# w_ff_out loaded on ScalarE's queue, two tiles of w_ff_in loaded ahead, and evictions placed between two high/low parts, in a float32 decoder block

## The chip, the cores and the metric

One core of one Trainium2 chip. The metric is the device time of one execution of the whole kernel in microseconds, the median of the runs.

## The reference

One decoder block on 512 tokens of width 1024, in float32. The part that this change touches is the last, the feed-forward stage with 4096 hidden columns:

```python
hf = rms_norm(x, norm_ff_pre)
ff = jnp.square(jax.nn.relu(hf @ w_ff_in)) @ w_ff_out
return x + rms_norm(ff, norm_ff_post)
```

Ahead of it stand the input projection, a chunked spatial gating, a windowed attention, their gated merge, and the product with w_o, whose normed result is added to x (the "mixing stage" below).

## The kernel before

It is written for each engine by hand: one program per engine, with semaphores between them, so the order on an engine is the order of the code.

**Three products for one.** To keep float32 accuracy on TensorE, each operand is split into a high part (a rounding to `F32R`, made by ScalarE: `w_hi`, `actB_hi`, `op_hi`) and a low part (the rest, made by VectorE: `w_lo`, ...). The helper `product` issues three 128x512 matmuls: high by high, high by low, low by high (L1368 to L1370). Weights come as 512 KB tiles into four buffers `w_raw[0..3]`; their high and low parts live in rings of four, `w_hi` and `w_lo`. Each such pair is a unit; `hi_made` and `lo_made` count them. Unit r may only be made once TensorE is through with unit r - 4, so a high part is always made four units ahead: when TensorE has finished unit r, `hi_ahead(r)` and `lo_ahead(r)` make unit r + 4.

**The feed-forward stage** runs in four chunks of 1024 hidden columns. A chunk has 22 units:

- eight units of "up": `acc` bank = one tile of w_ff_in by the activations (24 matmuls). ScalarE evicts each with a relu (L874), VectorE squares it (L1240) and forms sums and differences of the four column pairs. In chunk 0 the up units use four banks, later two.
- fourteen units of "down", 12 matmuls each: seven products P1, P5, P6, P7, P4, P3, P2 (the order of `PRODUCTS`) with two halves h each. It is a 2x2 block scheme with seven products in the place of eight. Their right operands are pieces of w_ff_out in `down_raw`, or differences T1 to T4 of such pieces, formed by VectorE in `weight_sum` (L1218) and kept in `down_raw` or in `t_raw`, which is another name of `w_raw[2:4]`.

P5, P7 and P3 stay in banks of their own over all chunks. P1, P6, P4 and P2 (`ROTATING`) take turns in banks `acc[0:2]`: each must be evicted into `sum1`, `sum6`, `sum4` or `sum2` before the next of them starts, and P2's before the next chunk's first up unit. Between P1 and P6, P6 and P4, P4 and P2 stands one resident product of two units, between P2 and the next chunk nothing. In chunk 0 ScalarE evicts them (copies at L894), in chunks 1 and 2 VectorE adds them (L1305), in the last chunk VectorE merges them with the other products (`merge`, L1224, and L1332, L1353). TensorE waits for that in `bank_free` and ahead of the up units (`taken`, counted per bank).

**What follows what around the change.** At every product, ScalarE calls `hi_ahead` for both halves and then evicts; VectorE calls `lo_ahead` for both halves, with the sums T2b, T3b, T4a, T4b among them, and then evicts or merges. Behind P2 the units made are the up units 2 and 3 of the next chunk.

Since T1, T2 and T4 occupy `w_raw[2:4]` during a chunk, the tiles of w_ff_in of chunks 1 to 3 all use buffers 0 and 1, one after the other: tile m waits for the low part of tile m - 2 (`load_up`). The blocks of w_ff_out, two rows of tiles or 1 MB each, are issued by SP between them (`load_down`, L506): behind each of tiles 2 to 5 of a chunk one block. All loads of weights are on SP's queue; ScalarE's queue carries two small loads at the start of the kernel.

In the mixing stage ScalarE makes the squares of the first half (`mix_square`, L806), then works through `WO_ORDER["act"]`.

Of the kernel before, what the change touches and what calls it, by code (L numbers as in the profile page):

```python
# [41 lines left out]
P = 128  # L42
D = 1024
# [205 lines left out]
def hybrid_block(nc, x, positions, w_in, ln_v_gain, ln_v_bias, w_spatial, b_spatial, sinks, w_a, w_b,  # L249
# [11 lines left out]
    with ExitStack() as ctx:  # L261
# [163 lines left out]
        def _(sp):  # L425
# [82 lines left out]
            for m in range(SLOTS):  # L508
                load_up(m)
            load_up(4)  # L510
            load_up(5)
            sp.wait_ge(a_lo, GROUPS)
            load_down(0, 0)
            load_down(0, 1)
            load_up(6)
            load_down(0, 2)
            load_up(7)
            load_down(0, 3)
            sp.wait_ge(pe_done, UNIT_DONE[U_FF - 1])
            sp.dma_start(g_ff_post[:], norm_ff_post[0:1, :].to_broadcast([P, D])).then_inc(g_ff_in, 16)  # L520
            for c in range(1, CHUNKS):
# [108 lines left out]
        def _(act):  # L630
# [171 lines left out]

            def mix_square(part, t, src, signal):
# [63 lines left out]
            for c in range(CHUNKS):  # L867
# [816 lines left out]
```

## Time and profile before

| | us |
|---|---|
| median of 3 runs (lowest to highest) | 811.88 (810.15 to 816.54) |
| the profiled execution | 810.79 |
| its span, first to last instruction | 809.1 |
| TensorE busy in it | 772.7 |
| VectorE busy | 529.7 |
| ScalarE busy | 364.8 |

The profile is of one execution. "PE" is TensorE, "DVE" VectorE, "ACT" ScalarE, "SPq" and "ACTq" are DMA issues on the queues of SyncE and ScalarE. In a timeline, an x with a number joins instructions of one kind; the time in brackets is how long the engine was idle before, with what released it. The granted clock is a share of 2.4 GHz.

### The profile page before, as it was taken

How to read it: one execution, taken by the hardware profiler on the slowest of the kernel's cores; microseconds unless marked ns; L12 is line 12 of the kernel's file. 1: busy time of each engine (PE TensorE's matmuls, PEld its weight loads, DVE VectorE, ACT ScalarE, POOL GpSimd, SP SyncE). 2: the span in 40 equal slices, each digit the busy share in tenths (PEclk: the TensorE clock that was granted, in tenths of full speed). 3: DMA queues.
4: the chain of work that ended last, by engine and by line, in shares of the span. 5: the costliest groups of instructions: out<-in, count | busy, mean ns of one | idle time of the engine just before them, and what ended most of it. 6: DMA issues, size and time to landing. Idle time of an engine off the chain costs nothing.

```text
span 809.1 us, 9921 instructions
## 1 busy us (share of the span) xinstructions
PE 772.7 (96%) x3640; PEld 645.1 (80%) x3640; DVE 529.7 (65%) x883; ACT 364.8 (45%) x609; POOL 58.3 (7%) x110
## 2 busy tenths in 40 slices
PE   7999999999999999999999999989996999979994
PEld 6888888888887888888888988778784887768873
DVE  5624667777775329766547698437962588547897
ACT  4523656656566552322245455334531344324532
POOL 3000000123222003000002000000000000000002
PEclk9999999999999999999999999999997999999998
DMA  8333222222123522353332440272008200270002
GB/s 286 127 108 89 69 79 78 79 79 79 53 79 107 179 79 86 96 211 109 114 89 82 168 141 1 99 242 76 1 0 308 83 26 1 81 257 27 0 1 104
DMA packets 91580, 80.29 MB, mean 99 GB/s; under 512 B 2832, under 2 KB 77584, under 8 KB 91536
## 3 DMA queue, kind: packets, MB, share of 16 engines
q1 hardware_dynamic: 90864, 79.70, 30.6%
q8 instruction: 27, 0.44, 0.2%
q14 instruction: 17, 0.14, 0.1%
q10 hardware_dynamic: 672, 0.01, 0.0%
HBM read 77.60 MB, written 2.10 MB: 99 GB/s over the span
## 4 chain that ended last, share of the span: by engine, by line
PE 86%; DVE 7%; DMA 3%; ACT 2%; issue 1%; SPq 0%; POOL 0%; DVEq 0%; POOLq 0%; ACTq 0%
PE acc L1368 25%; PE acc L1370 25%; PE acc L1369 25%; DMA w_raw<-in_w_ff_in 2%; PE aux L1370 2%; PE aux L1369 2%; PE aux L1368 2%; DVE w_lo L1201 1%; DMA w_raw<-in_w_in 1%; PE aux L1555 1%; PE aux L1481 1%; PE aux L1480 1%; PE aux L1490 1%; DVE w_lo L1197 1%; DVE sum L1224 1%; PE acc L1509 1%
## 5 line engine op out<-in xcount | busy, mean ns | idle before, releaser
L1368 PE MATMUL acc<-actB_hi,w_hi 128*128 128x512 f32 (+1 forms) x544 | 210.0, 386 | 17.4 <-DVE sum L1305 13.2
L1370 PE MATMUL acc<-actB_hi,w_lo 128*128 128x512 f32 (+1 forms) x544 | 207.2, 381 | 0.0
L1369 PE MATMUL acc<-actB_lo,w_hi 128*128 128x512 f32 (+1 forms) x544 | 207.1, 381 | 0.0
L919 DVE TENSOR_TENSOR w_lo<-w_raw,w_hi 128x1024 fp32r<-128x1024 f32 x72 | 87.8, 1223 | 83.9 <-ACT w_hi L636 83.1
L1368 PEld LDWEIGHTS acc<-actB_hi,w_hi 128*128 128x128 f32 x544 | 103.9, 191 | 37.1 <-DVE w_lo L1197 14.1
L1370 PEld LDWEIGHTS acc<-actB_hi,w_lo 128*128 128x128 f32 x544 | 103.7, 191 | 19.6
L1369 PEld LDWEIGHTS acc<-actB_lo,w_hi 128*128 128x128 f32 x544 | 104.0, 191 | 18.5
L636 ACT ACTIVATE w_hi<-w_raw 128x1024 fp32r<-128x1024 f32 x72 | 75.5, 1052 | 71.2 <-PE acc L1370 68.8
L1368 PE MATMUL acc<-w_hi,op_hi 128*128 128x512 f32 x160 | 62.5, 390 | 2.5 <-DVE sum L1305 1.3
L1368 PE MATMUL acc<-w_hi,actB_hi 128*128 128x512 f32 x160 | 62.7, 392 | 1.4 <-DVE actB_lo L929 1.3
L1370 PE MATMUL acc<-w_hi,op_lo 128*128 128x512 f32 x160 | 63.5, 397 | 0.0
L1369 PE MATMUL acc<-w_lo,op_hi 128*128 128x512 f32 x160 | 63.3, 396 | 0.0
L1370 PE MATMUL acc<-w_hi,actB_lo 128*128 128x512 f32 x160 | 62.3, 389 | 0.0
L1369 PE MATMUL acc<-w_lo,actB_hi 128*128 128x512 f32 x160 | 62.3, 389 | 0.0
L874 ACT ACTIVATE ff_act<-acc 128x512 f32<-128x512 f32 x32 | 19.1, 596 | 79.1 <-PE acc L1370 79.1
L1197 DVE TENSOR_TENSOR w_lo<-w_raw,w_hi 128x1024 fp32r<-128x1024 f32 x28 | 34.3, 1225 | 28.5 <-ACT w_hi L834 28.4
L1201 DVE TENSOR_TENSOR w_lo<-down_raw,w_hi 128x1024 fp32r<-128x1024 f32 x32 | 39.0, 1222 | 17.5 <-ACT w_hi L846 17.4
L1240 DVE TENSOR_TENSOR ff_act<-ff_act 128x512 f32<-128x512 f32 x32 | 22.0, 689 | 42.6 <-ACT ff_act L874 42.6
L846 ACT ACTIVATE w_hi<-down_raw 128x1024 fp32r<-128x1024 f32 x32 | 33.8, 1058 | 31.2 <-PE acc L1370 18.7
L745 ACT ACTIVATE probs<-scores_sb,neg_m 128x256 f32<-128x256 f32 (+1 forms) x64 | 30.1, 472 | 30.8 <-DVE sink_m L1068 30.8
L834 ACT ACTIVATE w_hi<-w_raw 128x1024 fp32r<-128x1024 f32 x28 | 29.6, 1056 | 30.4 <-DMA w_raw<-in_w_ff_in 21.0
L1368 PEld LDWEIGHTS acc<-w_hi,op_hi 128*128 128x128 f32 x160 | 30.7, 192 | 10.6 <-DVE w_lo L1201 2.1
(192 smaller groups left out, 1292.7 us busy)
## 6 DMA issues: line engine op xcount, KB each, us to landing
w_raw<-in_w_in SPq DMA_DIRECT2D x44, 512.0 KB, 3.8
w_raw<-in_w_ff_in SPq DMA_DIRECT2D x32, 512.0 KB, 4.1
down_raw<-in_w_ff_out SPq DMA_DIRECT2D x16, 1024.0 KB, 8.2
w_raw<-in_w_b SPq DMA_DIRECT2D x8, 512.0 KB, 3.6
w_raw<-in_w_a SPq DMA_DIRECT2D x8, 512.0 KB, 3.7
w_raw<-in_w_o SPq DMA_DIRECT2D x8, 512.0 KB, 3.7
x<-in_x SPq DMA_DIRECT2D x4, 512.0 KB, 7.4
x<-in_x SPq DMA_DIRECT2D x1, 2048.0 KB, 8.4
```

The lines of the kernel that those rows point to most:

```text
L636: nc.scalar.activation(w_hi[:, j], w_raw[:, j], ACT.Copy).then_inc(hi_made, 1)
L745: nc.scalar.activation(probs[:, h, off:], scores_sb[:, h, off:], ACT.Exp, bias=neg_m[:, h:h + 1], accum_out=denom[:, h:h + 1])
L834: nc.scalar.activation(w_hi[:, r % SLOTS], w_raw[:, j], ACT.Copy).then_inc(hi_made, 1)
L846: nc.scalar.activation(moving(w_hi, r % SLOTS), right_raw(name, h), ACT.Copy).then_inc(hi_made, 1)
L874: nc.scalar.activation(ff_act[:, m % 4], acc[:, bank], ACT.Relu).then_inc(relu_made, 1)
L919: nc.vector.tensor_tensor(w_lo[:, j], w_raw[:, j], w_hi[:, j].bitcast(F32), ALU.subtract).then_inc(lo_made, 1)
L1197: nc.vector.tensor_tensor(w_lo[:, r % SLOTS], w_raw[:, m if m < SLOTS else m % 2], w_hi[:, r % SLOTS].bitcast(F32), ALU.subtract).then_inc ...
L1201: nc.vector.tensor_tensor(moving(w_lo, r % SLOTS), right_raw(PRODUCTS[k], h), moving(w_hi, r % SLOTS).bitcast(F32), ALU.subtract).then_inc ...
L1240: nc.vector.tensor_tensor(f, f, f, ALU.mult).then_inc(sq_made, 1)
L1368: nc.tensor.matmul(o, a_hi, b_hi, start=first, stop=False)
L1369: nc.tensor.matmul(o, a_hi, b_lo, start=False, stop=False)
L1370: return nc.tensor.matmul(o, a_lo, b_hi, start=False, stop=last)
```

## The change

1. w_ff_out is issued from ScalarE. In chunk 0 two blocks go out before the squares of the mixing stage and two behind the last transposed tile; in chunks 1 to 3 all four behind the high part of tile 3, in front of the first relu.
2. Tiles 2 and 3 of w_ff_in of chunks 1 to 3 get buffers 2 and 3 (`up_slot`), free when the low parts of P4's two units of the chunk before are made. Tiles 4 and 5 then wait for tiles 0 and 1, tiles 6 and 7 for 4 and 5.
3. At every product an eviction stands between the two high parts (ScalarE) or the two low parts (VectorE). T3b and T4b stand behind the first low part. In the last chunk the merges of P1, P6, P7, P4 and P3 also stand between the two low parts; the gains of P4 stay behind both.

```diff
+def up_slot(m):
+
+    n = m % FF_UNITS
+    return n if n < SLOTS else n % 2
...
             def load_up(m):
-                if m < SLOTS:
+
+                c, n = divmod(m, FF_UNITS)
+                if n >= SLOTS:
+                    sp.wait_ge(lo_made, U_FF + ff_unit(m - 4 if n < 6 else m - 2) + 1)
+                elif c == 0:
                     slot_free(U_FF + m)
+                elif n < 2:
+                    sp.wait_ge(lo_made, U_FF + ff_unit(c * FF_UNITS - 2 + n) + 1)
                 else:
-                    before = m - 4 if m < 6 else m - 2
-                    sp.wait_ge(lo_made, U_FF + ff_unit(before) + 1)
-                load_columns(m if m < SLOTS else m % 2, w_ff_in_v, slice(m * P, (m + 1) * P))
-
-            def load_down(c, j):
-
-                if c:
-                    sp.wait_ge(lo_made, U_FF + item(c, 0))
-                elif j >= 2:
-                    sp.wait_ge(turned, T_FF + TT)
-                k = c * FF_UNITS + 2 * j
-                sp.dma_start(down_raw[:, j], w_ff_out_v[:, k:k + 2, :]).then_inc(down_loaded[j], 16)
...
+                    sp.wait_ge(lo_made, U_FF + product_item(c - 1, "P4", n - 2) + 1)
+                load_columns(up_slot(m), w_ff_in_v, slice(m * P, (m + 1) * P))
+
+            for c in range(CHUNKS):
                 for n in range(FF_UNITS):
                     load_up(c * FF_UNITS + n)
-                    if 2 <= n < 2 + PAIRS:
-                        load_down(c, n - 2)
...
+            def load_down(c, j):
+
+                k = c * FF_UNITS + 2 * j
+                act.dma_start(down_raw[:, j], w_ff_out_v[:, k:k + 2, :]).then_inc(down_loaded[j], 16)
+
+            act.wait_ge(a_lo, GROUPS)
+            load_down(0, 0)
+            load_down(0, 1)
+
...
+            act.wait_ge(turned, T_FF + TT)
+            load_down(0, 2)
+            load_down(0, 3)
+
...
                 for name in PRODUCTS:
-                    for h in range(2):
-                        hi_ahead(product_item(c, name, h))
+                    hi_ahead(product_item(c, name, 0))
                     if c == 0 and name in ROTATING:
                         dst = {"P1": sum1, "P6": sum6, "P4": sum4, "P2": sum2}[name]
                         for p in range(2):
                             act.wait_ge(pe_done, BANK_DONE[U_FF + product_item(c, name, 1), p])
                             nc.scalar.activation(dst[:, p], acc[:, p], ACT.Copy).then_inc(taken, 1)
+                    hi_ahead(product_item(c, name, 1))
+                    if name == "P2" and c < CHUNKS - 1:
+                        act.wait_ge(lo_made, U_FF + item(c + 1, 0))
+                        for j in range(PAIRS):
+                            load_down(c + 1, j)
...
-                    for h in range(2):
-                        at = FF_UNITS + 2 * PRODUCTS.index(name) + h
-                        for made in {8: ["T2b"], 9: ["T3b"], 10: ["T4a"], 11: ["T4b"]}.get(at, []):
-                            weight_sum(c, made)
-                        lo_ahead(item(c, at))
+                    at = FF_UNITS + 2 * PRODUCTS.index(name)
+                    for made in {8: ["T2b"], 10: ["T4a"]}.get(at, []):
+                        weight_sum(c, made)
+                    lo_ahead(item(c, at))
+                    for made in {8: ["T3b"], 10: ["T4b"]}.get(at, []):
+                        weight_sum(c, made)
...
+                    lo_ahead(item(c, at + 1))
+                    if last and name == "P4":
                         dve.wait_ge(ff_ready, 4)
```

On ScalarE, at the end of chunk 0 (P4, P3, P2) and the start of chunk 1, this stood there before; `w_hi<-w_raw` at L834 are the up tiles of chunk 1:

```order
L846 ACTIVATE w_hi<-down_raw 128x1024 x4
L894 ACTIVATE sum4<-acc 128x512 x2
L834 ACTIVATE w_hi<-w_raw 128x1024 x4
L894 ACTIVATE sum2<-acc 128x512 x2
L874 ACTIVATE ff_act<-acc 128x512
```

and this now (L854 and L842 are the old L846 and L834, L901 the old L894, L882 the old L874):

```order
L854 ACTIVATE w_hi<-down_raw 128x1024 x3
L901 ACTIVATE sum4<-acc 128x512 x2
L854 ACTIVATE w_hi<-down_raw 128x1024
L842 ACTIVATE w_hi<-w_raw 128x1024 x3
L901 ACTIVATE sum2<-acc 128x512 x2
L842 ACTIVATE w_hi<-w_raw 128x1024
L801 DMA down_raw<-in_w_ff_out 128x2x1024 x4
L882 ACTIVATE ff_act<-acc 128x512
```

One high part moved from in front of each pair of evictions to behind it, and four DMA issues came in before the first relu.

On VectorE, from P1 to the start of the next chunk, in chunk 1, this stood there before (L1218 are the sums T2b, T3b, T4a and T4b, L1201 and L1197 the low parts, L1305 the evictions):

```order
L1218 TENSOR_TENSOR w_raw<-down_raw,w_raw 128x1024
L1201 TENSOR_TENSOR w_lo<-w_raw,w_hi 128x1024
L1218 TENSOR_TENSOR down_raw<-down_raw 128x2x512
L1201 TENSOR_TENSOR w_lo<-w_raw,w_hi 128x1024
L1305 TENSOR_TENSOR sum1<-acc,sum1 128x512 x2
...
L1305 TENSOR_TENSOR sum4<-acc,sum4 128x512 x2
L1197 TENSOR_TENSOR w_lo<-w_raw,w_hi 128x1024 x4
L1305 TENSOR_TENSOR sum2<-acc,sum2 128x512 x2
L1240 TENSOR_TENSOR ff_act<-ff_act 128x512
```

and this now (L1230, L1213, L1209, L1318 and L1252 are the old L1218, L1201, L1197, L1305 and L1240):

```order
L1230 TENSOR_TENSOR w_raw<-down_raw,w_raw 128x1024
L1213 TENSOR_TENSOR w_lo<-w_raw,w_hi 128x1024
L1230 TENSOR_TENSOR down_raw<-down_raw 128x2x512
L1318 TENSOR_TENSOR sum1<-acc,sum1 128x512 x2
L1213 TENSOR_TENSOR w_lo<-w_raw,w_hi 128x1024
...
L1209 TENSOR_TENSOR w_lo<-w_raw,w_hi 128x1024 x3
L1318 TENSOR_TENSOR sum2<-acc,sum2 128x512 x2
L1209 TENSOR_TENSOR w_lo<-w_raw,w_hi 128x1024
L1252 TENSOR_TENSOR ff_act<-ff_act 128x512
```

The evictions of P1 stand one low part earlier, and so do those of P2.

## Rows read from the trace of the kernel before

**Rows 1.** The page: busy time of TensorE, its share of the span, instructions.
```profile
PE 772.7 (96%) x3640; PEld 645.1 (80%) x3640; DVE 529.7 (65%) x883; ACT 364.8 (45%) x609; POOL 58.3 (7%) x110
```

**Rows 2.** What TensorE waited for: us in total, times, longest us.
```profile
PE acc L1368 <- DVE sum L1305: 14.5, 4, 7.7
PE acc L1368 <- ACT sum L894: 4.2, 1, 4.2
...
PE acc L1368 <- DVE sum L1224: 1.2, 1, 1.2
```

**Rows 3.** Timeline of TensorE: start, duration, line, operation, [idle before, its releaser].
```profile
524.06 0.40 PE L1369 MATMUL acc<-w_lo,op_hi 128*128 128x512 f32 x1
524.29 0.40 PE L1370 MATMUL acc<-w_hi,op_lo 128*128 128x512 f32 x1
...
528.84 0.76 PE L1368 MATMUL acc<-actB_hi,w_hi 128*128 128x512 f32 x1 [4.15 <-ACT sum L894]
...
531.97 0.40 PE L1369 MATMUL acc<-actB_lo,w_hi 128*128 128x512 f32 x1
...
621.56 0.77 PE L1368 MATMUL acc<-actB_hi,w_hi 128*128 128x512 f32 x1 [7.74 <-DVE sum L1305]
...
627.62 0.39 PE L1370 MATMUL acc<-actB_hi,w_lo 128*128 128x512 f32 x1
...
713.35 0.77 PE L1368 MATMUL acc<-actB_hi,w_hi 128*128 128x512 f32 x1 [5.49 <-DVE sum L1305]
...
716.40 0.39 PE L1369 MATMUL acc<-actB_lo,w_hi 128*128 128x512 f32 x1
```

**Rows 4.** Stretches; behind busy times per engine: granted clock, DMA share, GB/s.
```profile
584.00:588.00 4.00, 3.36 (x15) 2.45 (x14) 4.00 (x5) 1.06 (x1) 0.00 (x0) 1.00 0.00 0
...
613.90:621.50 7.60, 0.00 (x0) 0.00 (x0) 2.35 (x4) 1.06 (x1) 0.00 (x0) 0.72 1.06 368
621.56:627.50 5.94, 5.94 (x14) 4.68 (x15) 0.45 (x1) 0.00 (x0) 0.00 (x0) 0.50 0.89 320
```

**Rows 5.** Timelines at the second boundary: ScalarE, then VectorE, then SP's queue.
```profile
608.37 1.06 ACT L834 ACTIVATE w_hi<-w_raw 128x1024 fp32r<-128x1024 f32 x1 [1.71 <-PE aux L1370]
...
618.50 1.06 ACT L834 ACTIVATE w_hi<-w_raw 128x1024 fp32r<-128x1024 f32 x1 [5.43 <-DMA w_raw<-in_w_ff_in]
...
620.73 1.28 DVE L1305 TENSOR_TENSOR sum<-acc,sum 128x512 f32<-128x512 f32 x2
...
611.13 0.58 SPq L506 DMA_DIRECT2D down_raw<-in_w_ff_out  x1
614.36 0.37 SPq L431 DMA_DIRECT2D w_raw<-in_w_ff_in  x1
```

**Rows 6.** Timelines at P6 of chunk 1: VectorE, then TensorE.
```profile
583.88 1.22 DVE L1201 TENSOR_TENSOR w_lo<-w_raw,w_hi 128x1024 fp32r<-128x1024 f32 x1
585.02 1.28 DVE L1305 TENSOR_TENSOR sum<-acc,sum 128x512 f32<-128x512 f32 x2
...
585.85 0.47 PE L1368 MATMUL acc<-w_hi,op_hi 128*128 128x512 f32 x1 [0.64 <-DVE sum L1305]
```

**Rows 7.** Timeline of VectorE in the last chunk.
```profile
777.84 1.23 DVE L1201 TENSOR_TENSOR w_lo<-w_raw,w_hi 128x1024 fp32r<-128x1024 f32 x1 [0.26 <-ACT w_hi L846]
...
783.32 1.23 DVE L1201 TENSOR_TENSOR w_lo<-down_raw,w_hi 128x1024 fp32r<-128x1024 f32 x1 [0.67 <-ACT w_hi L846]
...
798.97 0.68 DVE L1353 TENSOR_TENSOR sum<-acc,sum 128x512 f32<-128x512 f32 x1
```

**Rows 8.** The issues at L506 (min/median/max ns), their landing; timeline of ScalarE.
```profile
L506 SPq DMA_DIRECT2D down_raw<-in_w_ff_out x16: 469/582/2438, 440.6 to 713.0; - x16
...
DMA to landing us min/median/max: 6.1/8.2/10.3
...
421.18 0.60 ACT L806 ACTIVATE junk_wo<-acc 128x512 f32<-128x512 f32 x1 [0.84 <-PE acc L1370]
...
455.47 0.60 ACT L874 ACTIVATE ff_act<-acc 128x512 f32<-128x512 f32 x1 [4.72 <-PE acc L1370]
```

More of the change, by code:

```diff
@@ L99, in product_item, with up_loads @@
     return item(c, FF_UNITS + 2 * PRODUCTS.index(name) + h)
+def up_slot(m):
+    n = m % FF_UNITS
+    return n if n < SLOTS else n % 2
+def up_loads(m):
+    return U_FF // SLOTS + sum(up_slot(x) == up_slot(m) for x in range(m + 1))
 def ff_unit(m):
@@ L491, in load_up @@
             def load_up(m):
-                if m < SLOTS:
+                c, n = divmod(m, FF_UNITS)
+                if n >= SLOTS:
+                    sp.wait_ge(lo_made, U_FF + ff_unit(m - 4 if n < 6 else m - 2) + 1)
+                elif c == 0:
                     slot_free(U_FF + m)
-                else:
-                    before = m - 4 if m < 6 else m - 2
-                    sp.wait_ge(lo_made, U_FF + ff_unit(before) + 1)
-                load_columns(m if m < SLOTS else m % 2, w_ff_in_v, slice(m * P, (m + 1) * P))
-            def load_down(c, j):
-                if c:
-                    sp.wait_ge(lo_made, U_FF + item(c, 0))
-                elif j >= 2:
-                    sp.wait_ge(turned, T_FF + TT)
-                k = c * FF_UNITS + 2 * j
-                sp.dma_start(down_raw[:, j], w_ff_out_v[:, k:k + 2, :]).then_inc(down_loaded[j], 16)
[L508 to L521, printed above, removed]
+                elif n < 2:
+                    sp.wait_ge(lo_made, U_FF + ff_unit(c * FF_UNITS - 2 + n) + 1)
+                else:
+                    sp.wait_ge(lo_made, U_FF + product_item(c - 1, "P4", n - 2) + 1)
+                load_columns(up_slot(m), w_ff_in_v, slice(m * P, (m + 1) * P))
+            for c in range(CHUNKS):
                 for n in range(FF_UNITS):
                     load_up(c * FF_UNITS + n)
-                    if 2 <= n < 2 + PAIRS:
-                        load_down(c, n - 2)
+                if c == 0:
+                    sp.wait_ge(pe_done, UNIT_DONE[U_FF - 1])
+                    sp.dma_start(g_ff_post[:], norm_ff_post[0:1, :].to_broadcast([P, D])).then_inc(g_ff_in, 16)
             for n, t in enumerate((2, 3)):
@@ L826, in _ @@
                     hi_of(U_FF + t)
+            act.wait_ge(turned, T_FF + TT)
+            load_down(0, 2)
+            load_down(0, 3)
             def hi_up(m):
-                j = m if m < SLOTS else m % 2
-                act.wait_ge(w_loaded[j], 16 * (U_FF // SLOTS + 1 + (0 if m < SLOTS else (m - SLOTS) // 2 + 1)))
+                j = up_slot(m)
+                act.wait_ge(w_loaded[j], 16 * up_loads(m))
                 r = ff_unit(m)
@@ L1196, in lo_ahead @@
                     m = c * FF_UNITS + n
-                    nc.vector.tensor_tensor(w_lo[:, r % SLOTS], w_raw[:, m if m < SLOTS else m % 2],
+                    nc.vector.tensor_tensor(w_lo[:, r % SLOTS], w_raw[:, up_slot(m)],
                                             w_hi[:, r % SLOTS].bitcast(F32), ALU.subtract).then_inc(lo_made, 1)
@@ L1305, in _ @@
                             nc.vector.tensor_tensor(dst[:, p], acc[:, p], dst[:, p], ALU.add).then_inc(taken, 1)
-                    if not last:
-                        continue
-                    if name == "P1":
+                    if last and name == "P1":
                         merged_so_far()
@@ L1313, in _ @@
                             merge(sum6[:, p], acc[:, p], sum6[:, p], signal=taken)
-                    if name == "P6":
+                    if last and name == "P6":
                         for p in range(2):
@@ L1319, in _ @@
                         merge(sum1[:], acc[:, 2:4], sum6[:])
-                    if name == "P7":
+                    if last and name == "P7":
                         bank_done(name, 1)
@@ L1333, in _ @@
                             ins.then_inc(ff_ready, 1)
+                    if last and name == "P3":
+                        for p in range(2):
+                            bank_done(name, p)
+                            merge(sum1[:, p], aux[:, 2 + p], sum1[:, p], signal=ff_ready)
+                    lo_ahead(item(c, at + 1))
+                    if last and name == "P4":
                         dve.wait_ge(ff_ready, 4)
@@ L1339, in _ @@
                             gain(2 + p, sum4[:, p], 0, 2 + p)
-                    if name == "P3":
-                        for p in range(2):
-                            bank_done(name, p)
-                            merge(sum1[:, p], aux[:, 2 + p], sum1[:, p], signal=ff_ready)
+                    if last and name == "P3":
                         for p in range(2):
```

1 line of the change is left out of this document (removed).

## The prediction

> **What bounds the kernel now.** I read the page first, then what TensorE waits for, then the granted clock by stretches, then the timelines around the waits. TensorE is busy 96% of the span [rows 1]. What it waits for after the first 20 us is short [rows 2]: evictions of product banks into `sum` tiles, 14.5 us in 4 waits on VectorE (two at L1305 of about 0.64 us each, two large), 4.2 us in one wait on ScalarE (L894) and 1.2 us at L1224. The three large ones stand where a chunk of the feed-forward stage ends and the next begins: chunks 0 to 1, 1 to 2, 2 to 3. The timelines show 4.15, 7.74 and 5.49 us idle there, and behind each the matmuls start 0.43 us apart instead of 0.23 [rows 3].
>
> The clock explains the spacing: 0.50 granted (1.2 GHz) for the 5.94 us behind the second gap, against 1.00 (2.4 GHz) in a stretch with a 0.64 us gap [rows 4]. TensorE had been idle for 4 us and more before it fell, and stayed up through 0.64 us. The Trainium skill ("TensorE: Matmul & The Clock Gate", section "HAM oscillation — how this bites in real kernels") says that a TensorE left waiting for a DMA falls back to half clock and starts cold. By that rule, the trace agrees, at 0.50 behind all three large gaps. Were the small gaps left by this change to cost the clock too, by the price of the shortest stretch at half clock (1.5 us) twice, the sum below would be 3.0 us smaller.
>
> Why is the eviction late? Follow the second boundary [rows 5]. The chain reads backwards: TensorE starts at 621.56, 0.83 us behind the start of the P2 evictions (620.73); those stand on VectorE behind the low part of tile 3 of the next chunk, this behind its high part on ScalarE (618.50), this behind its DMA (idle 5.43 us, released by w_ff_in), and that DMA was only issued at 614.36, in a buffer that was free only then, behind 1 MB blocks of w_ff_out on the same queue (611.13). TensorE's own operands (tile 0) were ready long before. So a buffer wait and a transfer hold an eviction that has nothing to do with them.
>
> **The change, part by part.**
>
> *Tiles 2 and 3 ahead, blocks of w_ff_out off the queue.* Tiles 2 and 3 of chunks 1 to 3 go into buffers 2 and 3, free once the low parts of P4 exist; that is before P4 starts, six units of 2.77 us or 16.6 us ahead of the boundary (a unit of a product is 12 matmuls, 0.23 apart). Tiles 4 and 5 take the old place of 2 and 3. ScalarE's high parts no longer wait for a DMA there, and fall back into the rhythm of one per unit, 2.77 us.
>
> *Eviction between the two units.* At the boundary the P2 evictions now stand behind one high/low part, not two. Boundary 0 to 1 (ScalarE evicts): the high part of tile 2 is done about 1.3 us after the first half of P2; bank 0 is complete 1.4 us into the second half, eviction about 0.6 us; it ends before TensorE is through. Gap left: 0. Boundaries 1 to 2 and 2 to 3 (VectorE evicts): high part at 608.37 + 2.77 = 611.14, eviction 2.23 later with the low part between them (as 618.50 to 620.73 [rows 5]) = 613.37, TensorE 0.83 later = 614.20. Its own next place would be 621.56 − 7.91 = 613.65. Gap left: 0.55, with the restart 0.6. Bounds: 0 and 1.2 (the gap at L1224, [rows 2]); I take the 0.6 that the rows give.
>
> The terms [rows 3]; a gap costs its idle time plus 0.17 (524.29 to 528.84 is 4.55, less the usual 0.23, is 4.32, idle 4.15):
> - 0 to 1: 4.32, and 7 matmuls at half clock 3.13 − 7 × 0.23 = 1.52: 5.8.
> - 1 to 2: 7.91, and 14 such matmuls 6.06 − 3.22 = 2.84, less 0.6 left: 10.2.
> - 2 to 3: 5.66, and 7 such matmuls 3.05 − 1.61 = 1.44, less 0.6 left: 6.5.
>
> *P1 evictions before the low part of P6's second half.* In chunks 1 and 2 TensorE waits 0.64 us at P6 for them [rows 6]. They now start 1.14 us sooner, more than the wait: 2 × (0.64 + 0.17) = 1.6. What moves back is that low part: it now begins when two evictions (1.28) are through from 583.88, and takes 1.22, so it is there at about 586.4. P6 would start at 585.85 − 0.81 = 585.04 and its second half 2.77 later, 587.81. The cover is 1.4 us, so nothing new is late.
>
> *Last chunk.* The same move lets P6 begin 1.14 us sooner, but the end is not TensorE's: from 777.84 on VectorE breaks off only once until 798.97, where it begins the evictions of P2; it does not wait for TensorE there, it comes late to a finished bank [rows 7]. So only its idle bits count: 0.26 at 777.84 and 0.67 at 783.32, both waits for a high part. In the new order merges stand in those places, and TensorE is 1.14 us ahead with the operands: walking the chain in the new order with the same durations puts 798.97 at about 797.9. 1.1 us; bounds 0 and 1.4 (all of the gap before P6 and its refill).
>
> *Price of issuing from ScalarE.* Removed from SP: 16 issues that nobody would miss. Added to ScalarE: 16. Before the squares of the mixing stage two of them, about 2 × 0.58 us; ScalarE idles 0.84 us behind those squares, so some 0.3 us is pushed on [rows 8]. TensorE waited nowhere in that stretch [rows 2]; bounds 0 and 0.3, I take 0. Two more stand behind the last transposed tile, where ScalarE idles 4.72 us [rows 8]. In chunks 1 to 3 four stand between the high part of tile 3 and the first relu. One block has cost 0.47 to 2.44 us on SP's queue, median 0.58 [rows 8]; no block was ever issued from ScalarE, so its hold is bounded by 4 × 0.47 = 1.9 and 4 × 2.44 = 9.8, and I take 4 × 0.58 = 2.3. It begins 1.3 to 1.9 us behind the boundary; the relu is wanted at 5.5 and TensorE asks for its bank only at the third unit, 11.0. With a relu and its signal of 0.7, the hold may last 9.0 us and cost nothing. At 9.8 it costs 0.8 per boundary. A gain there is excluded, since ScalarE had no issue before. The blocks themselves are first read in the third unit, 16 us behind the boundary; 4 MB at the 360 GB/s or so of the boundaries (368 in [rows 4]) take 11.6.
>
> Sum: 5.8 + 10.2 + 6.5 + 1.6 + 1.1 = 25.2 us. The profiled execution took 810.79 (span 809.1 and 1.7 around it): 785.6. The median of the runs, 811.88, is 1.1 above it and the highest 816.54. The three boundaries cost 4.15, 7.74 and 5.49 idle for the same work, so part of that scatter is in the DMA wait that goes; I leave the 785.6 as the median too.
>
> **The rivals.**
> - *ScalarE is held by a full queue* (each issue as the dearest seen, 2.44). For: four in a row will meet more in flight than the blocks of before, which had a tile and a wait between them. Against: the median of 16 is 0.58. 0.8 × 3 = 2.4, and a late relu may return the two P6 gaps, 1.6: 787.9 to 789.6.
> - *Each block waits on ScalarE for the one before it to land* (the slower side). Landing takes 6.1 us at least [rows 8]: 3 × 6.1 + 0.6 = 18.9 of hold, relu done 1.3 + 18.9 + 0.7 = 20.9 behind the boundary, TensorE waits 9.9, and 2.8 of half clock: 12.7 × 3 = 38, so 824. It decides from 8.4 us per boundary on (25.2/3), a hold of some 15 us. Against it: SP was held 0.58 us by the median issue while the landing took 8.2 [rows 8].
> - *The transfers stay the bound.* If tile 3 still arrived at the boundary, sharing the engines with 4 MB, only the small terms would be won: 1.6 + 1.1, 808. Against: it is asked for 16.6 us ahead, with nothing else in flight. The Trainium skill ("DMA: Bandwidth & Descriptors", section "Issuing engines are not separate DMA queues") says that DMAs from any engine run on the same 16 engines and interleave. By that rule the second queue buys no transfer time at all; the trace has no load of this size on ScalarE's queue to test it.
> - *Half of it:* one boundary keeps a gap long enough for the clock to fall, some 6 us: 792.
>
> **How the numbers follow.** Forecast 0.80; queue-held 0.11; half 0.03; transfers still the bound 0.03; slower 0.03. The forecast's own band is 785.6 with 1.2 down (both left gaps vanish), 0.5 for the tail, and about 1.5 up (gaps of 1.2, tail 0). The range 783.0 to 789.5 leaves 0.9 for scatter below that and takes in the queue-held case. A measurement tells about 1% (8 us) from no change: faster by more than that 0.94, within it 0.03, slower 0.03.
>
> **What would show it.** TensorE's waits in the new profile: the L894-type wait gone, two of 0.4 to 0.6 us at the boundaries behind `sum`, none at P6 of chunks 1 and 2, about 0.1 or 0.3 in the last; clock 1.00 from the first units on; no ScalarE wait for w_ff_in in the stage; four block issues of about 0.6 us each in front of the first relu of chunks 1 to 3. Wrong would be: blocks issued in over 2.4 us each, a relu that TensorE waits for, or an idle VectorE between 783 and 798 in the last chunk.

## The result, and the profile after

| | before | changed |
|---|---|---|
| median of the runs (us) | 812.94 (810.15 to 816.54) | 785.36 (784.99 to 786.96) |
| ratio, with its 95% interval | | 0.9662 (0.962 to 0.9705) |
| the profiled execution | 810.79 | 784.99 |
| its span | 809.1 | 783.3 |

The medians are of four runs of each kernel. The forecast was 785.6. Two lines of the changed kernel's page, engines and the chain of waits, where TensorE stood at 772.7 us or 96% before [rows 1]:

```profile
PE 765.7 (98%) x3640; PEld 640.6 (82%) x3640; DVE 529.2 (68%) x883; ACT 365.2 (47%) x609; POOL 58.3 (7%) x110
...
PE 90%; DVE 7%; ACT 1%; DMA 1%; issue 0%; POOL 0%; SPq 0%; DVEq 0%; POOLq 0%; ACTq 0%
```

The work is the same: the count of matmuls is still 3640. Of the 7.0 us less of "busy", 5.8 are the matmuls that ran at half clock behind the three gaps before, by the terms of the prediction; the rest lies at the gaps that are gone and in the first 20 us. What TensorE waited for in the stage, of the rows that answer to [rows 2], is one line (L1382 is the old L1368, L1318 the old L1305):

```profile
PE acc L1382 <- DVE sum L1318: 0.8, 2, 0.4
```

and these are the two waits in the timeline, at the boundaries of chunks 1 to 2 and 2 to 3, where [rows 3] had 7.74 and 5.49:

```profile
607.32 0.47 PE L1382 MATMUL acc<-actB_hi,w_hi 128*128 128x512 f32 x1 [0.38 <-DVE sum L1318]
...
690.31 0.47 PE L1382 MATMUL acc<-actB_hi,w_hi 128*128 128x512 f32 x1 [0.39 <-DVE sum L1318]
```

The first boundary shows no gap at all. The granted clock, in the stretches around the second boundary and over everything from 540 us on (busy time and counts of each engine, then clock, DMA share, GB/s), against 0.50 in [rows 4]:

```profile
606.00:612.00 6.00, 5.62 (x26) 4.34 (x25) 3.00 (x4) 1.06 (x1) 0.00 (x0) 1.00 0.79 285
...
540.00:783.00 243.00, 232.38 (x1013) 190.09 (x1011) 189.19 (x234) 101.80 (x132) 4.52 (x10) 0.99 0.24 80
```

To give each term its measured size I set the two traces side by side at the first relu of each chunk. Before (the first relu of the stage, 455.47, is in [rows 8]):

```profile
536.07 0.60 ACT L874 ACTIVATE ff_act<-acc 128x512 f32<-128x512 f32 x1 [6.88 <-PE acc L1370]
...
630.11 0.60 ACT L874 ACTIVATE ff_act<-acc 128x512 f32<-128x512 f32 x1 [10.55 <-PE acc L1370]
...
720.48 0.60 ACT L874 ACTIVATE ff_act<-acc 128x512 f32<-128x512 f32 x1 [9.13 <-PE acc L1370]
```

and after:

```profile
455.37 0.60 ACT L882 ACTIVATE ff_act<-acc 128x512 f32<-128x512 f32 x1 [4.72 <-PE acc L1384]
...
530.07 0.60 ACT L882 ACTIVATE ff_act<-acc 128x512 f32<-128x512 f32 x1 [3.89 <-PE acc L1384]
...
613.05 0.60 ACT L882 ACTIVATE ff_act<-acc 128x512 f32<-128x512 f32 x1 [4.95 <-PE acc L1384]
...
696.03 0.60 ACT L882 ACTIVATE ff_act<-acc 128x512 f32<-128x512 f32 x1 [4.95 <-PE acc L1384]
```

| from the first relu of ... to the next | before | after | won | forecast |
|---|---|---|---|---|
| chunk 0 (holds boundary 0 to 1) | 80.60 | 74.70 | 5.90 | 5.8 |
| chunk 1 (P6 of chunk 1, boundary 1 to 2) | 94.04 | 82.98 | 11.06 | 0.8 + 10.2 |
| chunk 2 (P6 of chunk 2, boundary 2 to 3) | 90.37 | 82.98 | 7.39 | 0.8 + 6.5 |
| chunk 3, to the end of the span | 88.6 | 87.3 | 1.3 | 1.1 |

The differences add up to 25.7 of the 25.8 us between the two profiled executions (810.79 and 784.99); the last 0.1 came ahead of the stage (455.47 to 455.37).

### The profile page after: what moved, and what is told of

It reads as the page before. It is cut to its first block, busy times and chain, and to the rows that moved or that the text cites. A ratio compares the mean times of both kernels' runs of the same rounds, so it can differ in the third digit from the quotient of the medians.

```text
span 783.3 us, 9921 instructions
## 1 busy us (share of the span) xinstructions
PE 765.7 (98%) x3640; PEld 640.6 (82%) x3640; DVE 529.2 (68%) x883; ACT 365.2 (47%) x609; POOL 58.3 (7%) x110
## 4 chain that ended last, share of the span: by engine, by line
PE 90%; DVE 7%; ACT 1%; DMA 1%; issue 0%; POOL 0%; SPq 0%; DVEq 0%; POOLq 0%; ACTq 0%
PE acc L1382 26%; PE acc L1384 26%; PE acc L1383 26%; DVE w_lo L1213 2%; PE aux L1383 1%; PE aux L1384 1%; PE aux L1382 1%; DVE sum L1236 1%; PE aux L1569 1%; DMA g_pre<-in_norm_mix_pre 1%; PE aux L1495 1%; PE aux L1494 1%; PE aux L1504 1%; PE acc L1523 1%; PE acc L1520 1%; PE aux L1477 1%
## 5 line engine op out<-in xcount | busy, mean ns | idle before, releaser
L1382 PE MATMUL acc<-actB_hi,w_hi 128*128 128x512 f32 (+1 forms) x544 | 207.2, 381 | 0.8 <-DVE sum L1318 0.8
L1383 PE MATMUL acc<-actB_lo,w_hi 128*128 128x512 f32 (+1 forms) x544 | 205.0, 377 | 0.0
L1382 PEld LDWEIGHTS acc<-actB_hi,w_hi 128*128 128x128 f32 x544 | 102.4, 188 | 19.5 <-DVE w_lo L1209 1.6
L1382 PE MATMUL acc<-w_hi,actB_hi 128*128 128x512 f32 x160 | 62.7, 392 | 1.4 <-DVE actB_lo L941 1.3
L1382 PE MATMUL acc<-w_hi,op_hi 128*128 128x512 f32 x160 | 62.3, 390 | 0.1
L882 ACT ACTIVATE ff_act<-acc 128x512 f32<-128x512 f32 x32 | 19.1, 598 | 66.3 <-PE acc L1384 66.3
L1213 DVE TENSOR_TENSOR w_lo<-down_raw,w_hi 128x1024 fp32r<-128x1024 f32 x32 | 39.0, 1222 | 14.6 <-ACT w_hi L854 14.6
L854 ACT ACTIVATE w_hi<-down_raw 128x1024 fp32r<-128x1024 f32 x32 | 33.8, 1057 | 31.0 <-PE acc L1384 18.0
L1209 DVE TENSOR_TENSOR w_lo<-w_raw,w_hi 128x1024 fp32r<-128x1024 f32 x28 | 34.3, 1225 | 19.1 <-ACT w_hi L842 19.1
L1252 DVE TENSOR_TENSOR ff_act<-ff_act 128x512 f32<-128x512 f32 x32 | 22.0, 688 | 31.3 <-ACT ff_act L882 31.3
L842 ACT ACTIVATE w_hi<-w_raw 128x1024 fp32r<-128x1024 f32 x28 | 29.6, 1055 | 18.5 <-PE aux L1384 10.0
L1382 PEld LDWEIGHTS acc<-w_hi,op_hi 128*128 128x128 f32 x160 | 30.7, 192 | 7.5 <-issue 0.5
```

The costliest lines, as they stand in the source:

```text
L842: nc.scalar.activation(w_hi[:, r % SLOTS], w_raw[:, j], ACT.Copy).then_inc(hi_made, 1)
L854: nc.scalar.activation(moving(w_hi, r % SLOTS), right_raw(name, h), ACT.Copy).then_inc(hi_made, 1)
L882: nc.scalar.activation(ff_act[:, m % 4], acc[:, bank], ACT.Relu).then_inc(relu_made, 1)
L1209: nc.vector.tensor_tensor(w_lo[:, r % SLOTS], w_raw[:, up_slot(m)], w_hi[:, r % SLOTS].bitcast(F32), ALU.subtract).then_inc(lo_made, 1)
L1213: nc.vector.tensor_tensor(moving(w_lo, r % SLOTS), right_raw(PRODUCTS[k], h), moving(w_hi, r % SLOTS).bitcast(F32), ALU.subtract).then_inc ...
L1252: nc.vector.tensor_tensor(f, f, f, ALU.mult).then_inc(sq_made, 1)
```

## The experiments

### Which part carries the gain: the order, the loads, the queue

**The order alone** (e1_order): the kernel before with

```diff
-                    for h in range(2):
-                        hi_ahead(product_item(c, name, h))
+                    hi_ahead(product_item(c, name, 0))
                     if c == 0 and name in ROTATING:
...
+                    hi_ahead(product_item(c, name, 1))
```

and the same for VectorE's low parts, merges and sums.

> The kernel before with the new order of evictions alone; tiles and blocks are loaded as before. Theory (an eviction is late because it stands behind a high and a low part that wait for a transfer): only tile 2 is now in front of it. By the rows of before, tile 2's high part came at 522.89, 612.01 and 706.03, so the gaps left are about 0.2, 1.4 and 1.4 us: gains 5.6 + 9.3 + 5.6 at the boundaries, 1.6 at P6 and 1.1 in the last chunk, 23 us, about 788. Rival (the transfers themselves bound the boundary): tile 3 lands as late as before, so only 1.6 + 1.1 are won, about 808.

Measured: 788.42 us (787.42 to 789.5), ratio 0.9699 (0.9671 to 0.9726). TensorE's gaps in the timeline:

```profile
608.57 0.47 PE L1370 MATMUL acc<-actB_hi,w_hi 128*128 128x512 f32 x1 [1.30 <-DVE sum L1306]
...
692.65 0.47 PE L1370 MATMUL acc<-actB_hi,w_hi 128*128 128x512 f32 x1 [1.48 <-DVE sum L1306]
```

No gap at the first boundary, 1.30 and 1.48 at the others. The order alone, with every load as it was, brings 25 of the 28 us that lie, on the same chip, between the kernel before (813.11) and the kernel with all parts (785.28 with its blocks issued by SP, e4_sp below). Tile 3 still lands behind the boundary: its high part starts 2.7, 2.7 and 2.9 us behind the place where the matmuls of P2 end (2.6, 4.9 and 2.6 before), but no eviction stands behind it.

**The loads alone** (e2_loads): the changed kernel, evictions behind both halves again.

```diff
-                    hi_ahead(product_item(c, name, 0))
+                    for h in range(2):
+                        hi_ahead(product_item(c, name, h))
                     if c == 0 and name in ROTATING:
...
-                    hi_ahead(product_item(c, name, 1))
```

> The changed kernel with the old order of evictions: tiles 2 and 3 ahead and w_ff_out on ScalarE's queue, evictions behind both high or low parts. Theory: no wait for a transfer is left, but the eviction comes one unit late: gaps of about 2.0 us (chunk 0 to 1) and 3.3 us (twice), P6's two gaps and the last chunk's as before. Gains 3.9 + 7.4 + 3.8 = 15 us, about 796, and up to 799 if the clock falls behind the gaps of 3.3. Rival (the transfers are the bound, the order is small change): about 788.

Measured: 798.32 us (797.51 to 799.46), ratio 0.982 (0.9793 to 0.9848). The three gaps:

```profile
526.66 0.47 PE L1380 MATMUL acc<-actB_hi,w_hi 128*128 128x512 f32 x1 [1.78 <-ACT sum L902]
...
613.34 0.48 PE L1380 MATMUL acc<-actB_hi,w_hi 128*128 128x512 f32 x1 [3.16 <-DVE sum L1317]
...
700.05 0.48 PE L1380 MATMUL acc<-actB_hi,w_hi 128*128 128x512 f32 x1 [3.16 <-DVE sum L1317]
```

1.78, 3.16 and 3.16 us idle, where 2.0 and 3.3 were expected. So the loads are worth 15 us alone (813.11 to 798.32) and 3 us (788.42 to 785.28) once the order is right: the two parts shorten the same gap and don't add up.

**The queue alone** (e3_queue): the kernel before, with `load_down` moved from `sp.dma_start` to `act.dma_start` behind P2's evictions, and nothing else.

> The kernel before with w_ff_out alone moved to ScalarE's queue, behind the boundary; buffers and order as before. Theory (tile 3 was late because blocks of 1 MB were under way beside it, and they now start later): tile 3 lands in about 3.7 us as the other tiles do, in the place of 5.5 and 7.7: gaps of 2.5, 3.9 and 3.8 us, gain 13 to 14 us, about 797. Rival (a second queue buys no transfer time, and only buffers set when tile 3 lands): no gain, about 811.

Measured: 802.87 us (802.65 to 805.68), ratio 0.9871 (0.9846 to 0.9896). The gaps in its trace:

```profile
529.83 0.47 PE L1364 MATMUL acc<-actB_hi,w_hi 128*128 128x512 f32 x1 [2.60 <-ACT sum L886]
...
618.95 0.47 PE L1364 MATMUL acc<-actB_hi,w_hi 128*128 128x512 f32 x1 [4.00 <-DVE sum L1301]
...
707.94 0.48 PE L1364 MATMUL acc<-actB_hi,w_hi 128*128 128x512 f32 x1 [3.92 <-DVE sum L1301]
```

The gaps came as expected (2.5, 3.9 and 3.8 against 2.60, 4.00 and 3.92); the time did not, it is 6 us over. The expectation had taken the clock for recovered behind gaps of this length. The clock rows say otherwise; stretches of the idle time and of the matmuls behind it, at the first boundary:

```profile
527.20:529.80 2.60, 0.03 (x1) 0.00 (x1) 1.22 (x2) 1.66 (x3) 0.00 (x0) 1.00 0.20 52
529.83:530.50 0.67, 0.67 (x3) 0.59 (x4) 0.63 (x1) 0.35 (x1) 0.00 (x0) 1.00 0.91 265
530.50:531.50 1.00, 1.00 (x6) 0.77 (x5) 0.00 (x0) 0.00 (x0) 0.00 (x0) 0.78 1.11 401
531.50:532.50 1.00, 1.00 (x4) 0.80 (x3) 0.00 (x0) 0.00 (x0) 0.00 (x0) 0.50 1.02 401
```

The clock is full through the gap, full for the first 0.7 us of work, and then half. It fell behind all three gaps. A stretch of length L at clock g loses (1 - g) L, which is some 1.7 us behind each gap, 5.1 of the 6 us.

Tile 3 of the second boundary was issued at 611.85 here, and its high part starts on ScalarE 4.04 us later (7.78 in the kernel before, 610.72 to 618.50), with the issues of the blocks right behind it:

```profile
615.89 1.06 ACT L826 ACTIVATE w_hi<-w_raw 128x1024 fp32r<-128x1024 f32 x1 [1.66 <-DMA w_raw<-in_w_ff_in]
615.90 2.28 ACTq L785 DMA_DIRECT2D down_raw<-in_w_ff_out  x4
```

**The same loads, issued by SP** (e4_sp): the changed kernel with the blocks on SP's queue.

```diff
             for c in range(CHUNKS):
                 for n in range(FF_UNITS):
                     load_up(c * FF_UNITS + n)
+                    if n == 5:
+                        for j in range(PAIRS):
+                            load_down(c, j)
```

> The changed kernel with w_ff_out back on SP's queue, four blocks behind tile 5 of each chunk. Theory (which engine issues is of no account, only what is in flight ahead of the boundary; all six tiles are asked for before the blocks): 785 to 786, no difference from the changed kernel. Rival (ScalarE's queue is itself the gain): gaps come back at the boundaries or in the units after them, 788 or more.

Measured: 785.28 us (785.1 to 785.32), ratio 0.9655 (0.963 to 0.968). One line of TensorE's waits, the same as in the changed kernel:

```profile
PE acc L1379 <- DVE sum L1315: 0.8, 2, 0.4
```

In this kernel it is of no account which engine issues. What e3_queue won goes with the time at which the blocks start: beside or behind the high part of tile 3, no longer beside its transfer, which took 4.0 us at the second boundary in the place of 7.76. The buffers alone, with the blocks issued where they were, were not run.

**The order at P2 alone** (e6_p2_only): the kernel before with the new order at P2 only.

```diff
-                    for h in range(2):
-                        hi_ahead(product_item(c, name, h))
+                    hi_ahead(product_item(c, name, 0))
+                    if name != "P2":
+                        hi_ahead(product_item(c, name, 1))
...
+                    if name == "P2":
+                        hi_ahead(product_item(c, name, 1))
```

VectorE's low parts at P2 likewise.

> The kernel before with only P2's evictions placed between its two high or low parts; P1, P6, P4, the last chunk and all loads as before. Theory: the boundary terms of the order come alone: the time of the order-only kernel (788.4) plus what P6 (1.6) and the last chunk (1.1) are worth, 791; the trace shows gaps of 0.64, 0.64 and 1.24 us at P6 again and about 0, 1.3 and 1.5 at the boundaries. Rival (the other places are worth nothing, their time is given back at the end): 788.4 again.

Measured: 790.63 us (790.33 to 790.81), ratio 0.9724 (0.9691 to 0.9758). Its waits of TensorE:

```profile
PE acc L1374 <- DVE sum L1309: 4.2, 4, 1.5
...
PE acc L1374 <- DVE sum L1227: 1.2, 1, 1.2
```

The four at L1309 are 1.50 and 1.43 at the boundaries and 0.64 twice at P6; the 1.24 of the last chunk is back too. By the medians, 790.63 to 788.42, P6 and the last chunk are worth 2.2 us, but the two kernels ran on different chips and the runs of e1_order lie 2.1 us apart. By the two traces, from the first relu of the stage to the end, it is 333.5 us (455.31 to 788.8) against 330.3 (455.44 to 785.7): 3.2 us. The terms said 2.7. So the small places are worth 2 to 3 us, and one moved pair of evictions per chunk, P2's, carries 21 of the 28 us (811.64, the kernel before on the same chip, to 790.63).

### What is left at the boundaries

**P2's evictions ahead of both low parts** (e5_p2_first), in chunks 1 and 2:

```diff
+                    if 0 < c and not last and name == "P2":
+                        dst = {"P1": sum1, "P6": sum6, "P4": sum4, "P2": sum2}[name]
+                        for p in range(2):
+                            bank_done(name, p)
+                            nc.vector.tensor_tensor(dst[:, p], acc[:, p], dst[:, p], ALU.add).then_inc(taken, 1)
                     at = FF_UNITS + 2 * PRODUCTS.index(name)
```

> The changed kernel with the P2 evictions of chunks 1 and 2 ahead of both low parts. Theory: what is left at these boundaries (0.38 and 0.39 us idle, each with 0.17 of restart) is the low part in front of the eviction: both gaps go, 1.1 us, 784.2. Rival (it is the hand-over between TensorE and VectorE, which no order shortens): 785.3.

Measured: 785.12 us (783.6 to 785.94), ratio 0.9656 (0.962 to 0.9692). The median shows next to nothing, so the trace has to tell. In it TensorE has no gap left in the whole stage. From the first relu of the stage to the end it is 326.67 us (456.23 to 782.9) against 327.93 in the changed kernel (455.37 to 783.3): 1.3 us won, where 1.1 was expected. The profiled execution began its stage 0.9 us later. That has nothing to do with the edit: it is a start in which the clock drops to half, and three of the fourteen profiled executions have one. The row of e3_queue, which also stood at 0.81 in 16 to 24 us:

```profile
8.00:16.00 8.00, 4.68 (x21) 3.59 (x21) 6.19 (x6) 4.68 (x7) 0.80 (x2) 0.77 1.04 408
```

In 8 to 16 us the granted clock was 0.77 in e3_queue, 0.79 in e5_p2_first and 0.74 in e9_hold12. Just before, TensorE had been idle for 2.56, 2.46 and 2.27 us until x came; in the eleven other traces it was idle there for 0.95 to 2.17 us and the clock stayed at 1.00. The three began the stage at 458.01, 456.23 and 457.61 us, the eleven at 455.2 to 455.7. So a start of this kind costs 0.8 to 2.6 us against the middle of the eleven (455.44) and is a part of the scatter between runs; nothing was changed to test that.

### Whose is the end

**The last instructions of VectorE in another order** (e7_tail):

```diff
             for p in range(2):
                 dve.wait_ge(pe_done, BANK_DONE[UNITS - 1, p])
                 nc.vector.tensor_tensor(sum2[:, p], acc[:, p], sum2[:, p], ALU.add).then_inc(ff_ready, 1)
                 gain(6 + p, sum2[:, p], 0, p)
+            for p in range(2):
                 dve.wait_ge(rstd_ff, 3 + p)
```

VectorE in the last chunk of the changed kernel, the merges of P1, and the two evictions of P2, each with the updates behind it:

```profile
743.84 2.48 DVE L1236 TENSOR_TENSOR sum<-acc,sum 128x512 f32<-128x512 f32 x4
...
773.28 0.68 DVE L1367 TENSOR_TENSOR sum<-acc,sum 128x512 f32<-128x512 f32 x1
...
775.73 1.42 DVE L1373 SCALAR_TENSOR_TENSOR x<-down_raw,rstd,x 128x512 f32<-128x512 f32 x2 [1.04 <-POOL rstd L547]
777.06 0.68 DVE L1367 TENSOR_TENSOR sum<-acc,sum 128x512 f32<-128x512 f32 x1
...
779.43 1.42 DVE L1373 SCALAR_TENSOR_TENSOR x<-down_raw,rstd,x 128x512 f32<-128x512 f32 x2 [0.96 <-POOL rstd L547]
```

From 743.84 to 773.28 it never waits. TensorE's last matmul starts at 772.85. Behind that VectorE waits twice, 1.04 and 0.96 us, for a power that GpSimd makes (`rstd`) before it can update x.

> The changed kernel with the last instructions of VectorE in another order: both evictions of P2 with their gains first, then both updates of x, where before the second eviction stood behind the first update. Theory (the end is VectorE's and its order's, not TensorE's, which is through at 773.2 of 783.3): the second eviction starts at about 774.7 in the place of 777.06, the end comes 2.2 us sooner, 783.1. Rival (the end is a fixed distance behind TensorE's last matmul): 785.3, no difference.

Measured: 783.81 us (783.43 to 785.76), ratio 0.9649 (0.9613 to 0.9684). VectorE's end in its trace:

```profile
774.66 0.68 DVE L1367 TENSOR_TENSOR sum<-acc,sum 128x512 f32<-128x512 f32 x1
...
777.84 1.41 DVE L1374 SCALAR_TENSOR_TENSOR x<-down_raw,rstd,x 128x512 f32<-128x512 f32 x2 [0.44 <-POOL rstd L547]
```

The second eviction is at 774.66, as expected, the end 1.6 us sooner, not 2.2. The expectation had asked for more than there was: what the new order fills is VectorE's idle time, 1.04 + 0.96 = 2.00 us before, of which 0.44 is left in front of the last update. The end is that of VectorE's chain, with GpSimd's power in it; moving the second eviction and its gain forward moves the end, with TensorE as it was.

### How long ScalarE may be held

**Eight, and twelve, more copies in front of the first relu** (e8_hold8, e9_hold12), with 8 or 12 in `range`:

```diff
                         for j in range(PAIRS):
                             load_down(c + 1, j)
+                        act.wait_ge(g_ff_in, 16)
+                        for k in range(8):
+                            nc.scalar.activation(g_ff_post[:], g_ff_post[:], ACT.Copy).then_inc(act_step, 1)
+                            act.wait_ge(act_step, 8 * c + k + 1)
```

and one wait on VectorE in the last chunk, so that `g_ff_post` isn't read before the last copy.

> The changed kernel with eight more copies on ScalarE (an idle 128x1024 tile onto itself, one after the other, 1.1 us each) behind the block issues and in front of the first relu of chunks 1 to 3; nothing else is changed. Theory (ScalarE may be held 9 us there at no cost): 8.8 us of hold, the relu starts about 9.9 behind the boundary, TensorE does not wait for it: 785.3, at most 1.6 more if VectorE's delay brings P6's gaps back. Rival (the cover was never there, any hold in front of the relu shows): some 8 us per chunk, 795 or more.

Measured: 787.29 us (787.23 to 788.36), ratio 0.9687 (0.9654 to 0.9721). ScalarE at the second boundary, which lies at 608.43 here:

```profile
610.48 8.71 ACT L909 ACTIVATE g_ff_post<-g_ff_post 128x1024 f32<-128x1024 f32 x8 [1.28 <-DVE w_lo L1213]
619.22 0.60 ACT L882 ACTIVATE ff_act<-acc 128x512 f32<-128x512 f32 x1
```

and TensorE at the third up unit of each chunk:

```profile
536.29 0.47 PE L1387 MATMUL acc<-actB_hi,w_hi 128*128 128x512 f32 x1 [0.87 <-ACT ff_act L882]
...
619.97 0.47 PE L1387 MATMUL acc<-actB_hi,w_hi 128*128 128x512 f32 x1 [0.42 <-ACT ff_act L882]
...
703.44 0.47 PE L1387 MATMUL acc<-actB_hi,w_hi 128*128 128x512 f32 x1 [0.20 <-ACT ff_act L882]
```

I had left the four block issues out of the hold: the relu starts 10.8 us behind this boundary, not 9.9 (11.2 and 10.6 at the others), so this kernel stands just beyond the cover, and the gaps are 0.87, 0.42 and 0.20 us: 1.5 us, 2.0 with their restarts. That is the price measured. The start of the relu less the gap puts the edge of the cover at a relu 10.3 to 10.4 us behind the boundary; the prediction had it at 10.3, a hold of 9.0 that begins 1.3 behind. P6's gaps did not come back.

> The changed kernel with twelve copies (not eight) on ScalarE in front of the first relu of chunks 1 to 3. Eight gave a relu that began 10.8 us behind the boundary and gaps of 0.87, 0.42 and 0.20 us at the third unit. Theory (beyond the cover each us costs a us, and the clock falls with gaps of some us): 4.35 us later, gaps of 4.6 to 5.2, 13.5 us more and up to 2.8 of half clock each: 801 to 809. Rival (the loss is made up in the units after): 790 or less.

Measured: 806.18 us (805.67 to 809.34, 10 runs), ratio 0.9934 (0.9915 to 0.9953). TensorE at the same places:

```profile
542.95 0.76 PE L1387 MATMUL acc<-actB_hi,w_hi 128*128 128x512 f32 x1 [5.24 <-ACT ff_act L882]
...
633.10 0.74 PE L1387 MATMUL acc<-actB_hi,w_hi 128*128 128x512 f32 x1 [4.61 <-ACT ff_act L882]
...
722.59 0.77 PE L1387 MATMUL acc<-actB_hi,w_hi 128*128 128x512 f32 x1 [4.59 <-ACT ff_act L882]
```

That is 14.4 us idle, and most of the rest of the 21 us is half clock behind these gaps (0.50 in the first 2.9 to 3.4 us). The condition of the slower rival is real: held long enough in front of this relu, ScalarE gives back four fifths of the gain (21 of 27 us, by 811.91 and 785.22 on the same chip). The change stays some 8 us from that edge: with its issues as they are, eight copies of 8.71 us together overshot it by 0.20 to 0.87.

### The clock behind a gap of 3 us

**The loads-alone kernel once more** (e12_loads_look), unchanged: a second profiled execution of it. The granted clock of the first profile, e2_loads, in stretches behind each of its gaps:

```profile
526.66:530.00 3.34, 3.34 (x15) 2.75 (x16) 0.63 (x1) 0.34 (x1) 0.00 (x0) 1.00 0.96 374
...
613.34:616.00 2.66, 2.66 (x12) 2.17 (x13) 0.45 (x1) 0.00 (x0) 0.00 (x0) 1.00 1.03 422
...
700.05:703.00 2.95, 2.95 (x8) 2.32 (x9) 0.45 (x1) 0.00 (x0) 0.00 (x0) 0.57 1.02 421
```

Two gaps of 3.16 us, and full clock behind one, half behind the other (0.57 in the mean of the stretch).

> The kernel with loads ahead and the old order once more, one look. In its first profile two gaps of 3.16 us had different sequels: the clock stayed at 1.00 behind one and fell to half behind the other. If it is chance how the clock answers a gap of this length, another execution shows another pattern (both, neither, or the other way round), and its time moves by 1.5 us per fall. Rival (the place in the program decides): the same pattern again, full clock at chunk 1 to 2 and half at 2 to 3.

Measured, one execution: 799.22 us. The gaps are the same to 0.01 us:

```profile
613.36 0.54 PE L1380 MATMUL acc<-actB_hi,w_hi 128*128 128x512 f32 x1 [3.16 <-DVE sum L1317]
...
701.64 0.47 PE L1380 MATMUL acc<-actB_hi,w_hi 128*128 128x512 f32 x1 [3.16 <-DVE sum L1317]
```

the clock is not:

```profile
613.00:617.00 4.00, 3.64 (x9) 2.96 (x10) 0.81 (x2) 0.00 (x0) 0.00 (x0) 0.58 1.02 406
...
703.00:707.00 4.00, 4.00 (x14) 3.12 (x13) 0.00 (x0) 0.00 (x0) 0.00 (x0) 0.65 1.02 419
```

This time it fell behind both. With gaps alike to a hundredth and the program the same, the place alone does not decide it; the runs of this kernel (797.5 and 797.6, 799.0 to 799.5) lie one fall, some 1.5 us, apart. Over all fourteen traces, with the waits for x at the start: behind gaps of 2.17 us and less it never fell, behind 3.92 and more always; between, it fell behind 2.27, 2.46, 2.56 and 2.60, and behind three of the four of 3.16. What decides the fourth these runs don't show.

### Both finds together

**P2 first and the new end** (e10_both), beside the changed kernel once more on the same chip (e11_changed_again).

> The changed kernel with both finds together: P2's evictions of chunks 1 and 2 ahead of both low parts, and VectorE's last instructions in the new order. Theory: the two lie in different places and add up; from the first relu of the stage to the end it was 327.9 us in the changed kernel, and is 1.26 + 1.6 less, 325.0; the time 782.5. Rival (one takes the other's gain): 783.7.

> The changed kernel itself once more, on the same chip as the version with both finds, so that the two can be compared: 785 to 786; 327.9 us from the first relu to the end.

Measured: 782.33 us (781.77 to 782.64, 5 runs), ratio 0.9638 (0.9615 to 0.9661), against 785.22 us (784.81 to 786.92), ratio 0.9679 (0.9655 to 0.9704). From the first relu to the end it is 325.0 us (455.67 to 780.7) against 328.0 (455.52 to 783.5). The two add up, 2.9 us below the changed kernel and 29.6 below the kernel before on the same chip (811.91).

## Why the prediction was right, point by point

**The gaps and their terms.** Right in place and size, as the table above shows: no term is off by more than 0.3 us. The gap left at two boundaries was put at 0.55 and is 0.38 and 0.39 idle with 0.17 of restart: the same. That the median met the forecast too needs a word: the sum was taken off the one profiled execution (810.79), and the median of before stands 2.1 above it (812.94). The medians fell by 27.6 us, 1.8 more than the two profiled executions. The prediction let the median be 785.6 because a part of the scatter lay in the DMA wait that goes. The records agree: the runs of before spread over 6 us, those of the changed kernel over 2, and the tile of the second boundary was 7.76 us under way in the trace of before and 5.6 in that of e1_order, with the same loads. But no experiment took this scatter apart, so that the median of the changed kernel came out within 0.3 us of the forecast is in part luck.

**Why the eviction was late.** The chain was right (eviction behind low part, behind high part, behind a DMA), and e1_order shows it: with the order alone 1.30 of the 7.74 us are left though tile 3 still lands behind the boundary. But one reading in it was wrong. I took the issue at 614.36 for tile 3's. It is tile 4's. Tile 3's was issued one before, at the time when its buffer came free:

```profile
610.72 0.37 SPq L431 DMA_DIRECT2D w_raw<-in_w_ff_in  x1
```

and the chain of the kernel before has its journey (start, duration):

```profile
610.72 7.76 DMA w_raw<-in_w_ff_in
```

So "only issued at 614.36" fails: it was issued at 610.72 and was 7.76 us under way, beside blocks of 1 MB, where other tiles take about 4 (landing time, median 4.1 on the page); at the first boundary it was 5.55 us under way beside such blocks. At the second boundary the transfer was half of the delay, not the buffer alone. The sum didn't need that sentence, since it took the whole wait as gone. A forecast of a kernel with only the buffers or only the queue changed would have been off by it; e3_queue measures the queue's share: 3.7 us less idle at that boundary, 1.6 at each of the others.

**What carries the gain.** The prediction listed tiles ahead and order as two parts and summed over boundaries, which hid that either one alone removes most of the same gap: order alone 25 us, loads alone 15, both 28. The order is the part that counts.

**P6 and the last chunk.** Right: 1.6 and 1.1 forecast; together 2.2 by the medians of e6_p2_only and e1_order and 3.2 by their traces, and the last chunk 1.3 by the table. The claim that the end is VectorE's and not TensorE's was argued in the prediction and is shown by e7_tail.

**The price on ScalarE.** Four issues at 0.58 us were forecast. Measured, of the 16 issues:

```profile
L801 ACTq DMA_DIRECT2D down_raw<-in_w_ff_out x16: 374/492/664, 415.7 to 691.5; - x16
```

0.49 in the median, 0.66 at most, none of the 2.44 that the first rival feared. And they don't stand behind the activation in front of them, as the prediction placed them:

```profile
607.04 1.06 ACT L842 ACTIVATE w_hi<-w_raw 128x1024 fp32r<-128x1024 f32 x1 [1.72 <-PE acc L1384]
607.06 2.10 ACTq L801 DMA_DIRECT2D down_raw<-in_w_ff_out  x4
```

The four are issued from 607.06 to 609.16 while the activation of 607.04 runs to 608.10. So the hold begins 0.3 us ahead of this boundary (607.32), not 1.3 to 1.9 us behind it; that step was wrong, on the safe side. The 0.3 us that I had pushed on in the mixing stage, bounded at 0 and 0.3, is not there: the square that waits for TensorE is idle 0.84 before it as in [rows 8]. The end of the cover, a relu 10.3 us behind the boundary, is shown by e8_hold8, and the price beyond it by e9_hold12.

**The rivals.** A full queue: no. Serial landings: no (four issues took 2.10 us); that a long hold would have cost what it says is borne out by e9_hold12. Transfers still the bound: no, ScalarE waits for no w_ff_in in the stage. Half of it: no, the gaps left are 0.38 and 0.39. The rule of the Trainium skill on issuing engines ("DMA: Bandwidth & Descriptors", "Issuing engines are not separate DMA queues") could not be tested by the trace of before; e4_sp agrees with it, 785.28 us from SP against 785.36 from ScalarE.

**The clock.** The step "stayed up through 0.64 us, fell after 4 us" was right and too coarse. For this change nothing hung on the range between, but my expectation for e3_queue did and was 6 us off. Falls behind gaps of 2.27 to 2.60 us are in three traces. The rule of the Trainium skill ("TensorE: Matmul & The Clock Gate", "HAM oscillation — how this bites in real kernels") that a TensorE left waiting starts at half clock again holds behind the long gaps, and e2_loads and e12_loads_look show that a gap of 3.16 us may go either way.

## What to carry to other kernels

When a bank is handed over with nothing between its last use and its next, look at what stands in front of the eviction on the evicting engine, and put the eviction in front of work that is due later; that order alone, with no load touched, brought nine tenths of what order, loads, buffers and queue bring together, and its place at P2 three quarters. Edits that shorten the same wait are measured one by one before anyone adds them up. At the end of a kernel, ask again which engine the end belongs to: here TensorE was done 10 us before it, and one exchange among the last instructions of VectorE, which filled its waits for GpSimd, was worth 1.4 to 1.6 us.

## What was not expected of the hardware

- The clock can fall after the work has begun again: in e3_queue it was 1.00 through a gap of 2.60 us and the first 0.7 us behind it, then 0.50.
- It also fell at the start of the kernel, behind waits for x of 2.27, 2.46 and 2.56 us in three executions, and not behind 0.95 to 2.17 us in eleven. The stage began 0.8 to 2.6 us later in the three.
- The same gap of 3.16 us was followed by full clock once and by half clock three times, in two executions of one program.
- A DMA issue on ScalarE's queue runs beside an activation: four issues within 2.10 us, half of that time under an activation of 1.06.
- GpSimd's two small operations before the last update took 0.60 and 0.94 us in e7_tail, and 0.19 and 0.56 for the tile before; VectorE worked beside both pairs, on its updates beside the slow one, on an eviction and a multiply beside the other. Without that difference, 0.8 us, the last update would not have had to wait its 0.44 us; the rest of the miss of 0.6 lies in the forecast. What makes the difference was not tested.
